# The first modulation row of a two-block transformer kernel, split in half by features

## The reference

```
m = (silu(c) @ w_mod + b_mod)            # w_mod is 1024 x 6144; c is one vector
sh1, sc1, g1, sh2, sc2, g2 = split(m)    # the same for c_ctx, the second vector
h  = rms_norm(x,   norm_mix_g) * (1 + sc1)  + sh1
hc = rms_norm(ctx, norm_mix_g) * (1 + csc1) + csh1
a, g, q, k, v = split(h @ w_in)          # five parts, each 1024 x 512
k_c, v_c = split(hc @ w_in[:, k and v])
y_conv = silu(layer_norm(conv31(a * sigmoid(g))))
y_attn = neighbourhood attention of q over k, v and k_c, v_c
x = x + g1 * (concat(y_conv, y_attn) @ w_out)
```

## Time and profile before

| | us |
|---|---|
| median of 3 runs | 1705.87 |
| range | 1704.35 to 1707.75 |
| the profiled execution, its own time | 1706.17 |
| its span in the trace | 1704.3 |

### The profile page before, as it was taken

How to read it: one execution, slowest core, us unless ns; L and a number is a source line. 1 busy time by engine, 2 the same in 40 slices (tenths; PEclk the granted TensorE clock), 3 DMA queues, 4 the chain that set the end, 5 groups by cost and what they waited for, 6 DMA issues and landing times.

```text
span 1704.3 us, 21470 instructions
## 1 busy us (share of the span) xinstructions
PE 1390.7 (82%) x8860; PEld 849.1 (50%) x8860; DVE 534.4 (31%) x902; ACT 390.5 (23%) x581; POOL 138.8 (8%) x117
## 2 busy tenths in 40 slices
PE   6999996677577666766775766798999999999999
PEld 4886542122122212211221222376799998989997
DVE  2785410000000000000000000058365557835554
ACT  2516200000000000000000000057443346843332
POOL 3430000000000000000000000004500000720000
PEclk9999998777877768777778878999999999999999
DMA  9778699999999999999999999982145444325552
GB/s 357 284 286 317 263 398 429 430 428 428 430 427 429 429 427 430 428 428 430 427 428 429 429 428 428 429 320 99 66 182 193 176 156 154 135 99 198 198 181 90
DMA packets 83758, 542.06 MB, mean 318 GB/s; under 512 B 6664, under 2 KB 12137, under 8 KB 57082
## 3 DMA queue, kind: packets, MB, share of 16 engines
q1 hardware_dynamic: 80096, 535.93, 77.3%
q0 software_dynamic: 1888, 5.04, 1.0%
q10 hardware_dynamic: 1722, 0.35, 0.1%
HBM read 540.22 MB, written 1.08 MB: 318 GB/s over the span
## 4 chain that ended last, share of the span: by engine, by line
DMA 47%; PE 45%; DVE 4%; ACT 2%; issue 1%; POOL 1%; SPq 0%; ACTq 0%; DVEq 0%; POOLq 0%
DMA ring<-in_w_up 23%; DMA ring<-in_w_down 22%; PE bank L1428 10%; PE bank L1429 10%; PE bank L1430 10%; PE bank L1826 3%; PE bank L1845 3%; DMA ring<-in_a_w_in 2%; PE bank L1713 2%; DMA ring<-in_w_mod 1%; PE bank L1694 1%; PE bank L1458 1%; POOL ring_parts L798 1%; PE bank L2098 1%; PE bank L1686 1%
## 5 line engine op out<-in xcount | busy, mean ns | idle before, releaser
L1826 PE MATMUL bank<-ring,low 128*32 128x512 f32 x2016 | 323.2, 787 | 152.8 <-DMA ring<-in_w_up 122.6
L1826 PEld LDWEIGHTS bank<-ring,low 128*32 128x32 f32 x2016 | 67.6, 132 | 388.9 <-DMA ring<-in_w_up 194.5
L1845 PE MATMUL bank<-ring,low 128*32 128x512 f32 x976 | 164.7, 809 | 95.1 <-DMA ring<-in_w_down 88.0
L1176 ACT ACTIVATE low<-bank 128x512 f32<-128x512 f32 x16 | 9.6, 597 | 841.7 <-PE bank L1826 841.7
L965 ACT ACTIVATE ring_parts<-ring 128x4096 fp32r<-128x4096 f32 (+3 forms) x46 | 151.8, 3301 | 203.2 <-DMA ring<-in_mlp_w_down 100.2
L2155 DVE TENSOR_TENSOR ring_parts<-ring,ring_parts 128x4096 fp32r<-128x4096 f32 (+2 forms) x35 | 148.5, 4244 | 140.9 <-ACT ring_parts L965 140.9
L1429 PE MATMUL bank<-feat_parts,ring_parts 128*128 128x256 f32 x640 | 181.1, 283 | 0.0
L1430 PE MATMUL bank<-feat_parts,ring_parts 128*128 128x256 f32 x640 | 181.1, 283 | 0.0
L1428 PE MATMUL bank<-feat_parts,ring_parts 128*128 128x256 f32 x608 | 173.0, 285 | 5.2 <-DVE feat_parts L2128 2.6
L2527 DVE TENSOR_TENSOR low<-low,bank 128x512 f32<-128x512 f32 x16 | 11.0, 687 | 471.5 <-PE bank L1826 471.5
L1845 PEld LDWEIGHTS bank<-ring,low 128*32 128x32 f32 x976 | 31.3, 130 | 210.4 <-DMA ring<-in_w_down 137.2
(11 more groups left out here) (414 smaller groups left out, 1972.3 us busy)
## 6 DMA issues: line engine op xcount, KB each, us to landing
ring<-in_w_gate SPq DMA_DIRECT2D x64, 2048.0 KB, 25.7
ring<-in_w_up SPq DMA_DIRECT2D x62, 2048.0 KB, 23.7
ring<-in_w_down SPq DMA_DIRECT2D x61, 2048.0 KB, 26.2
ring<-in_mlp_w_up SPq DMA_DIRECT2D x16, 2048.0 KB, 7.9
ring<-in_mlp_w_down SPq DMA_DIRECT2D x16, 2048.0 KB, 7.9
ring<-in_w_mod SPq DMA_DIRECT2D x8, 2048.0 KB, 14.5
ring<-in_w_mod SPq DMA_DIRECT2D x8, 768.0 KB, 13.6
ring<-in_w_in SPq DMA_DIRECT2D x3, 2048.0 KB, 10.9
```

The lines of the kernel that those rows point to most:

```text
L1826: last = pe.matmul((GATE if i < 4 else UP)[32 * j:32 * j + 32, :], xsT[:, k, :], held(n, 2)[:, kk, 512 * j:512 * j + 512], start=(k == 0), ...
L1845: last = pe.matmul(TURN[32 * g:32 * g + 32, :], hidT[:, c, 32 * j:32 * j + 32], down_row(n, c, d), start=(j == 0 and c < 2), stop=(j == 3 ...
```

## The change

1. Row 0 of the modulation is cut into two equal halves of the features (`HEAD_K = KD // 2`), each over the whole contraction, loaded as eight pieces of 512 KB each, into ring slots 0 and 1 (half "a") and 2 and 3 (half "b"). Half "a" gives the first four feature blocks, half "b" the last four.
2. SP's order becomes: half "a"; the first two quarters of `a`'s weights; the first half of `g`'s; half "b"; the rest of `a`; the rest of `g`; the context; then `q`, `k`, `mods[1, 0]`, `mods[1, 1]`.
3. TensorE multiplies `a` and `g` for the first half of the contraction, with half "b" of the modulation between the parts of `g`, and then both for the second half. The transposes of the context move behind `g`. `rel` and `cw`, two small steps, move ahead of the token transposes. More `keep_clock` calls stand between the parts of half "a".
4. All four low quarters of `a` are POOL's. `x_low` writes the scaled input to SBUF (`x_plain`) and subtracts there, so that this subtraction has both inputs in SBUF.
5. `q` and `k` get high parts in quarters; low parts: `q` two quarters on POOL and a half on DVE, `k` four quarters on POOL. Their projections wait quarter by quarter.
6. `mods[1, 0]` is multiplied behind `q` instead of ahead of it. The small loads on ACT's queue move behind the high part of `k`.

```diff
-        HEAD_K = 6
+        HEAD_K = KD // 2
...
-            if name in "gqk":
-                mods[1, i - 1] = mod_chunk(1, i - 1)
+            for kp in {"q": (0, 1), "k": (2,)}.get(name, ()):
+                mods[1, kp] = mod_chunk(1, kp)
...
+            for k in range(KD):
+                first_row("a", k)
+            part(proj["a"], 0, 2, sem("a_first"))
+            part(proj["a"], 2, 4, sem("a_second"))
+            part(proj["g"], 0, 4, sem("g_first"))
+            for k in range(KD):
+                first_row("b", k)
+            for n in (proj["a"], proj["g"]):
+                part(n, 4, KD, slot_full[slot(n)])
             sp.dma_start(ctxt, I["ctx"][0].rearrange("(t p) d -> p t d", p=P)).then_inc(sem("ld_ctx"), 16)
-            begun = [proj["q"], mods[1, 0], proj["k"], mods[1, 1]]
+            begun = [proj["q"], proj["k"], mods[1, 0], mods[1, 1]]
...
+            for i in range(4):
+                quarter_low("a", i, (sem("w_high"), 1) if i == 3 else (sem("part_high"), QUARTER_HIGH["a"] + i + (i > 1)))
+            for i in range(2):
+                quarter_low("q", i, (sem("part_high"), QUARTER_HIGH["q"] + i))
+            for i in range(4):
+                quarter_low("k", i, (sem("w_high"), 4) if i == 3 else (sem("part_high"), QUARTER_HIGH["k"] + i))
...
+            act.wait_ge(sem("a_first"), 16)
+            quarter_high("a", 0)
+            act.wait_ge(sem("A1"), 2)
+            input_high(0, 0)
+            act.wait_ge(sem("a_second"), 16)
+            quarter_high("a", 1)
+            input_high(0, 1)
+            act.wait_ge(sem("g_first"), 16)
+            act.wait_ge(chunk_used, last_user(proj["g"], high_slot(proj["g"])))
+            gate_half_high(0)
+            act.wait_ge(*loads(proj["a"]))
+            quarter_high("a", 2)
+            act.wait_ge(sem("A1"), 5)
+            input_high(0, 2)
+            quarter_high("a", 3)
+            input_high(0, 3)
+            act.wait_ge(*loads(proj["g"]))
+            gate_half_high(1)
             act.wait_ge(sem("ld_ctx"), 16)
             rms("rc", ctxt, xn, D)
...
+            turn_tokens(xn, "xT", ready="rx_xn")
+            mod_first("a", (2, 3))
+            banks.wait_free(pe, "g1")
+            keep_clock(bk("g1"), 4)
+            mod_first("a", (4, 5))
+            keep_clock(bk("g1"), 4)
+            mod_first("a", (6, 7))
+            keep_clock(bk("g1"), 3)
             mod_turn_first("a")
-            keep_clock(bk("mod0b"), 20)
...
+            for i in range(2):
+                pe.wait_ge(sem("quarter_low"), i + 1)
+                pe.wait_ge(*drained(f"xT{i}"))
+                pair_tiles("a", i, range(4))
+            banks.wait_free(pe, "g0")
+            pe.wait_ge(sem("half_low"), 1)
+            pair_tiles("g", 0, range(4))
+            mod_first("b", range(0, 4))
+            pair_tiles("g", 1, (0, 1))
+            mod_first("b", range(4, KD))
+            pair_tiles("g", 1, (2, 3))
+            mod_turn_first("b")
+            keep_clock(bk("mod0b"), 8)
...
-            def x_low(who, i, name):
+            def x_low(who, i):
+                name = f"{('xT', 'cT')[who]}{i}"
                 dve.wait_ge(sem("hx_hi"), 4 * who + i + 1)
...
+                y = x_plain[who][:, 2 * i:2 * i + 2, :]
+                for kk in range(2):
+                    k = 2 * i + kk
+                    last = dve.tensor_scalar(y[:, kk, :], bk(name)[:, kk * T:(kk + 1) * T], A1[:, who, k:k + 1],
+                                             shift1[:, who, k:k + 1], ALU.mult, ALU.add)
+                link(last)
+                dve.tensor_tensor(hx[who][1][:, 2 * i:2 * i + 2, :], y, hx[who][0][:, 2 * i:2 * i + 2, :].bitcast(F32),
+                                  ALU.subtract).then_inc(banks.drain_sem(name), 1)
...
+            mod_vectors_first("a")
+            x_low(0, 0)
+            x_low(0, 1)
+            gate_half_low(0)
+            mod_vectors_first("b")
+            x_low(0, 2)
+            x_low(0, 3)
+            gate_half_low(1)
```

More of the change, by code:

```diff
@@ L410, in loads @@
             if slot(n) == X_SPARE:
-                return slot_full[X_SPARE], 16 * len(spare)
+                return slot_full[X_SPARE], 16 * (1 + len(spare))
             if slot(n) == X_REST:
                 return slot_full[X_REST], 16 * len(REST)
-            return slot_full[slot(n)], 16 * sum(1 + (m == mods[0, 4]) for m in range(n + 1) if slot(m) == slot(n)) + 32 * (slot(n) in HEAD_FULL)
+            before = sum(s == slot(n) for s, _ in HEAD_FULL + TAIL_FULL)
+            return slot_full[slot(n)], 16 * (before + sum(1 for m in range(n + 1) if slot(m) == slot(n)))
         def last_user(n, s):
             return max([m + 1 for m in range(n) if slot(m) == s or m in early_split and high_slot(m) == s
-                        or s in HEAD_SLOTS.get(m, ())], default=0)
+                        or s in FIRST_MOD_SLOTS.get(m, ())], default=0)
         def split_no(n):
@@ L1007, in _, with input_high @@
-            inputs_high(0, "xT", a_quarter)
-            for half in range(2):
-                act.wait_ge(*((sem("g_first"), 16) if half == 0 else loads(proj["g"])))
-                if half == 0:
-                    act.wait_ge(chunk_used, last_user(proj["g"], high_slot(proj["g"])))
-                act.activation(half_of(high(proj["g"], SLOT), half), half_of(loaded(proj["g"], SLOT), half), ACT.Copy)\
-                    .then_inc(sem("w_high" if half else "a_high"), 1)
+            def input_high(who, i):
+                name = ("xT", "cT")[who]
+                act.wait_ge(*banks.filled(f"{name}{i}"))
+                for k in (2 * i, 2 * i + 1):
+                    last = act.activation(hx[who][0][:, k, :], bk(f"{name}{i}")[:, (k % 2) * T:(k % 2 + 1) * T], ACT.Identity,
+                                          bias=shift1[:, who, k:k + 1], scale=A1[:, who, k:k + 1])
+                last.then_inc(sem("hx_hi"), 1)
@@ new lines, in quarter_high, with gate_half_high @@
+            def quarter_high(name, i):
+                n = proj[name]
+                act.activation(quarter_of(high(n, SLOT), i), quarter_of(loaded(n, SLOT), i), ACT.Copy)\
+                    .then_inc(sem("w_high" if i == 3 else "part_high"), 1)
+            def gate_half_high(half):
+                n = proj["g"]
+                act.activation(half_of(high(n, SLOT), half), half_of(loaded(n, SLOT), half), ACT.Copy)\
+                    .then_inc(sem("w_high" if half else "part_high"), 1)
@@ L1019, in _, with weights_high_quarters @@
-            weights_high(proj["q"])
-            inputs_high(1, "cT")
-            act.dma_start(rel_scratch, rel_rows[0:HEADS, :]).then_inc(sem("rel_saved"), 16)
+            def weights_high_quarters(name):
+                n = proj[name]
+                act.wait_ge(*loads(n))
+                act.wait_ge(chunk_used, last_user(n, high_slot(n)))
+                for i in range(4):
+                    quarter_high(name, i)
+            weights_high_quarters("q")
+            act.wait_ge(sem("A1"), 6)
@@ L1023, in _ @@
+            for part in "ab":
+                act.wait_ge(*drained(f"modT0{part}"))
+            act.wait_ge(*banks.filled("cT3"))
+            for i in range(4):
+                input_high(1, i)
             for i in range(2):
@@ L2245, in _ @@
-            x_low(0, 3, "xT")
-            n = proj["g"]
-            for half in range(2):
-                dve.wait_ge(*((sem("w_high"), split_no(n) + 1) if half else (sem("a_high"), 4)))
-                dve.tensor_tensor(half_of(low_part(n, SLOT), half), half_of(loaded(n, SLOT), half),
-                                  half_of(high(n, SLOT), half).bitcast(F32), ALU.subtract).then_inc(sem("g_low"), 1)
+                y = x_plain[who][:, 2 * i:2 * i + 2, :]
[3 more added lines that the diff above has]
+                                             shift1[:, who, k:k + 1], ALU.mult, ALU.add)
@@ L2255, in _ @@
+            dve.wait_ge(sem("A1"), 6)
+            for part in "ab":
+                dve.wait_ge(*drained(f"modT0{part}"))
             for i in range(4):
-                x_low(1, i, "cT")
+                x_low(1, i)
             dve.wait_ge(sem("pad_zero"), 1)
```

288 lines of the change are left out of this document (106 added, 182 removed).

## The result

| | median us | range, runs | ratio to before, 95% interval |
|---|---|---|---|
| before | 1705.53 | 1704.35 to 1707.75, 4 | |
| changed kernel | 1731.88 | 1729.02 to 1734.24, 4 | 1.0153 [1.0140, 1.0166] |

The change makes the kernel 26 us slower. The forecast was 1700.0, in a range of 1698.0 to 1706.5, with a chance of 0.07 for slower: it was wrong in sign and 32 us off. The profiled execution took 1732.88 (span 1731.1).

What follows compares the result with a forecast made beforehand. TensorE bounds the stretch from `k` to the end of `v`. `k` 6.2 us earlier, less 0.3 for refills, gives 5.9 off the profiled 1706.17: 1700.3, as a median 1700.0; range 1698.0 to 1706.5 (8 in 10).

Steps and rivals of the forecast that it cites:

- What bounds the kernel: From `k` to the end of `v` only TensorE binds; the worth is how much earlier `k` begins, 6.2 us.
- row 0 term: Modulation at the start: half "a" done at 23.5, so the first `a` product at 27.9 instead of 34.6.
- I take DVE first: In `x_low`, DVE's subtraction starts before POOL's quarter and loses nothing; POOL first would lose 2.2 us at each place.
- Rivals 1 and 2: POOL wins `x_low`'s races: clock holds, 1704.4 (chance 0.14, one lost race included); or clock falls, 1708.4 (0.11).
- rival 2: POOL wins at `x_low` and TensorE's clock falls: 5.9 - 4.4 - 4.0 = -2.5, 1708.4; chance 0.11.
- photo finish: At `x_low`, POOL's quarter starts 2.05 after ACT's input step begins, DVE's subtraction 2.09: called near even.
- Is everything else there at 60.4?: At `q`'s start, the other engines' operands are ready; `q` starts at 60.4 against 68.51, `k` at 75.9.
- Rival 4: Late weights: slack of `k` (0.8) and `v` (1.0) may be gone; gain about 4, 1702; chance 0.10.
- Moves of `rel`, `cw` and of the small loads cost nothing: DVE idles beside the moved `rel` and `cw`; the small loads fall into ACT's wait between `k` and `v`.
- I let them end at 18.6: Token transposes in row 0, 1.97 long, no longer wait for the second pair and end at 18.6.
- Slack of `v` 1.0: POOL's low part of `v` ends at 99.8, `v` is due at 100.8; slack falls from 6.2 but covers.
- Rival 3: Row 0's 512 KB loads are slower, 299 GB/s: half "b" 3.9 late, gain 1.8, 1704.1; chance 0.06.

Runs made afterwards that it cites:

- two runs with `k` at 97.5 and 97.6: Changed kernel without `q`'s first-tile wait for the eighth low quarter, 1724.94 us; changed kernel with 22 idle-product calls instead of 9 and 8, 1730.18 us.
- five mends, later bias loads: Changed kernel with PSUM copy, no eighth-quarter wait of `q`, sigmoids first, `rel`/`cw` behind transposes, bias loads only after `v`'s weights land: 1703.83 us, 0.9996.
- last mended: Five mends and later bias loads, plus `v`'s load before `mods[1, 2]`, second row 0 pair before token transposes, no idle products between later pairs: 1699.66 us, 0.9962.
- the clean one: The tightened-start kernel of 1699.66 us, edits tested singly: SBUF copy back gave 1706.43 us; `rel` and `cw` ahead of the token transposes again, 1702.36.
- all five mends: Changed kernel with PSUM copy, no eighth-quarter wait of `q`, sigmoids before context steps, `rel`/`cw` behind transposes, bias loads before `v`'s low part: 1714.79 us.

## Why the prediction was wrong, by its steps

**What bounds the kernel: right in the main.** The loss stands ahead of the output projection, as the forecast's worth did, and most of it ahead of `k` (19.6 of 26). But "if `v` and the convolution then keep pace" was no small condition: two runs with `k` at 97.5 and 97.6 differ by 5.2 through the waits behind `v`.

| | before | forecast | changed | five mends, later bias loads | last mended |
|---|---|---|---|---|---|
| first `a` product | 34.6 | 27.9 | 34.78 | 30.86 | 26.56 |
| second half of `a` | 47.33 | 47.1 | 58.67 | 50.23 | 45.94 |
| `q` | 68.51 | 60.4 | 80.51 | 63.47 | 59.19 |
| `k` | 82.14 | 75.9 | 101.76 | 78.73 | 74.45 |
| `v` | 107.2 | 100.8 | 127.30 | 104.67 | 99.53 |
| median | 1705.5 | 1700.0 | 1731.9 | 1703.8 | 1699.7 |

What failed first is the list of waits, the five below. With them out, and the bias loads where they do no harm, the steps are as long as forecast but all lie 3 to 4 us late, `k` 3.4 ahead of before instead of 6.2. That is the second thing that failed, the row 0 term. The last kernel is 1.2 to 1.5 ahead of the forecast at each line only because it has a tighter start than the change.

**"I take DVE first": wrong**, at both places, by 0.1 us. Rivals 1 and 2 had the price (2.2 each; the subtraction took 2.1 longer), the idle stretches (3.4 each; 3.38 and 3.60) and the low clock. Measured: 9.1 in the changed kernel, 6.8 in the clean one, against the 8.4 of rival 2. "POOL's own start-up lies inside its stamp" was no reason for VectorE. And the photo finish was set up from two different steps: 2.05 for GpSimd from ScalarE's first input step, 2.09 for VectorE from its second. At the first one the trace of the kernel before has

```profile
33.05 0.69 DVE L2217 TENSOR_TENSOR feat_parts<-bank,feat_parts 128x512 fp32r<-128x512 f32 x1
```

which is 2.19 behind ScalarE's 30.86, and 0.14 behind GpSimd's 32.91. In the changed kernel it is 2.16 (29.69 to 31.85) against 2.04.

**"Is everything else there at 60.4?": wrong, the largest miss.** I asked when operands are ready, not when the bank is free. "ACT's eight context steps, two sigmoids and first quarter take about 7.4 from the start of `q`" put the sigmoids behind a start that waits for them. Price: 8.0 (the low clock behind the wait included). Nor did I read the index in `q`'s wait: 6.9 with the clock behind it. Rival 4 named a late low part, but of `k` and `v`, and gave it 2.0.

**"Moves of `rel`, `cw` and of the small loads cost nothing": wrong for the first.** I named VectorE as the cover, and looked at neither the load of `conv_w` nor TensorE itself: 2.7 in the clean kernel; in the changed one the gain from undoing it (1.0) drowns in the noise. The move of ScalarE's small loads was not tested by itself.

**Row 0, "I let them end at 18.6": wrong by 4.4.** The sum took the pair of blocks and the transposes at the full rate that the kernel before has from 15.5 on. The new order stays at half rate until 23.2, its transposes take 1.7 longer, `rel` takes 1.88 instead of 1.03 ahead of them, and they end at 23.0. In the run with the five mends and the later bias loads this term alone is left, 3 us. (The unit in "24 tiles of 3 products at 0.12 are 2.88" is wrong too: it is 24 products; the 2.88 is right.)

**Slack of `v` 1.0: nearly right in size, wrong in what queues behind.** In the run with the later bias loads TensorE waits 0.8 for it. `q` and `k` are loaded late (slot 2, DMA engines empty from 44 to 51.5), but ScalarE's high part of `q` (67.18) waits for TensorE there, not for the load. The six bias loads behind `v`'s low part, which stand in no step of mine, cost 4.6. The experiment that moved them also shows that they can cost 11 in the wrong place.

**Rival 3, smaller loads: didn't come.** From 13 to 26 us the pieces of 512 KB move 379 GB/s with all five mends in, before 389, and TensorE never waits for a piece of row 0.

**Chances.** Slower had 0.07. The lost race had its chances, 0.25 for rivals 1 and 2 together; the other four waits (sigmoids, `q`'s index, `conv_w`, bias loads) had been given nothing, so they added nothing to it. The error is that the cover of each moved step was checked against one resource.

What is not settled: what decides when TensorE leaves the half rate between 15 and 26 us, and whether `v`'s load first is worth anything. In the last kernel `v` starts 7.7 ahead of before (107.2 to 99.53), while the profiled execution is 6.4 shorter (1706.17 to 1699.75). The other 1.3 go at the first expert products, in the chain of before and of the last kernel:

```profile
219.36 13.98 PE bank L1826 x128
```

```profile
211.77 15.20 PE bank L1832 x128
```

The second is 1.2 longer, with a granted clock of 0.51 from 210.8 to 214.3.

## What to carry to other kernels

When a step is moved up, list for its first instruction everything that it waits for: operands, the bank or buffer that it writes and who empties it, the number on each semaphore; then what stands behind it in each queue, small loads included. Where two engines meet within 0.1 us at a shared port, take the losing order as the forecast or make the order certain. Small loads that slow the large ones beside them belong where no large load is waited for.

## What the runs showed of the hardware

- A 128x512 subtraction with both inputs in SBUF takes 0.69 us alone or when it starts 0.1 first, and 2.78 to 2.79 when GpSimd's 2.35 us instruction, both inputs in SBUF too, began 0.1 earlier. In the other order GpSimd's takes 2.84.
- The bias loads move 1.26 MB in all. While they were under way beside 2 MB loads, all loads together moved 231 to 244 GB/s with the DMA engines 1.01 to 1.02 busy; without them 401 to 420.
